# Softmax band selected into 128 columns, parted again on GpSimd behind the transpose, and convolution steps spread over the recurrence

## The reference, cut to what matters

```python
kb, vb = band(k), band(v)                    # block n-1 and block n: 256 keys
s = jnp.einsum('bnqhgd,bnshd->bhgnqs', q, kb) * (B_HEAD_DIM ** -0.5)
dist = q_idx + BLOCK - s_idx                 # 128 x 256
mask = (dist >= 0) & (dist < WINDOW)         # and no key before the first
s = s - slopes * dist
s = jnp.where(mask, s, -jnp.inf)
m = jnp.maximum(jnp.max(s, axis=-1), sink)
p = jnp.exp(s - m)
p = p / (jnp.sum(p, axis=-1) + jnp.exp(sink - m))
o = jnp.einsum('bhgnqs,bnshd->bnqhgd', p, vb)
```

## Time and profile before

| | us |
|---|---|
| median of 3 runs | 1089.53 (1089.48 to 1092.77) |
| the profiled execution, as timed | 1090.27 |
| its span, first to last instruction | 1088.5 |
| TensorE busy | 1064.2 (98%) |
| VectorE busy | 688.7 (63%) |
| ScalarE busy | 532.7 (49%) |
| GpSimd busy | 115.9 (11%) |
| granted TensorE clock | 0.999 |

### The profile page before, as it was taken

The page is one execution under the profiler, slowest core; times in us unless marked ns, Lnnn a source line. Parts: engine busy times, 40 slices in busy tenths (PEclk is TensorE's granted clock), DMA queues, the critical chain, the costliest instruction groups (busy, mean ns, idle before and its releaser), DMA issues.

```text
span 1088.5 us, 19513 instructions
## 1 busy us (share of the span) xinstructions
PE 1064.2 (98%) x7212; PEld 846.5 (78%) x7212; DVE 688.7 (63%) x2081; ACT 532.7 (49%) x1557; POOL 115.9 (11%) x152
## 2 busy tenths in 40 slices
PE   7999999999999999999999999999999999999997
PEld 5877787778778787777887878787787878787885
DVE  5285959584665747576365665757537575758565
ACT  4557675754636454363354535435344555564300
POOL 3413132134100000020000000002000000002210
PEclk9999999999999999999999999999999999999999
DMA  8967475665553626253562551715454343622432
GB/s 282 315 209 262 163 274 195 243 208 183 201 205 109 237 73 235 87 185 98 175 228 93 165 215 46 265 49 185 132 179 157 126 157 128 215 73 63 137 116 77
DMA packets 58430, 183.55 MB, mean 169 GB/s; under 512 B 8480, under 2 KB 21216, under 8 KB 45024
## 3 DMA queue, kind: packets, MB, share of 16 engines
q1 hardware_dynamic: 58192, 182.05, 48.7%
q10 hardware_dynamic: 144, 0.26, 0.1%
HBM read 138.22 MB, written 44.07 MB: 167 GB/s over the span
## 4 chain that ended last, share of the span: by engine, by line
PE 65%; DVE 6%; DMA 2%; issue 1%; ACT 0%; SPq 0%; DVEq 0%
PE bank L849 33%; PE bank L900 10%; PE bank L1137 4%; PE bank L957 2%; PE bank L990 2%; PE bank L972 2%; PE bank L1107 1%; PE bank L1120 1%; PE bank L1117 1%; PE bank L1121 1%; DVE y_cols L1797 1%; DVE y_step L1793 1%; PE bank L1030 1%; PE bank L1045 1%; PE bank L1115 1%
## 5 line engine op out<-in xcount | busy, mean ns | idle before, releaser
L849 PE MATMUL bank<-xr,w 128*128 128x512 f32 x2496 | 653.9, 405 | 7.4 <-DVE xr L1534 7.4
L849 PEld LDWEIGHTS bank<-xr,w 128*128 128x128 f32 x2496 | 449.8, 189 | 101.7 <-issue 9.8
L900 PE MATMUL bank<-wo,y_split 128*128 128x512 f32 x432 | 114.4, 404 | 0.0
L900 PEld LDWEIGHTS bank<-wo,y_split 128*128 128x128 f32 x432 | 77.0, 189 | 14.6 <-issue 0.7
L1582 DVE SCALAR_TENSOR_TENSOR kq<-conv_in,convw_all,kq 128x512 f32<-128x512 f32 x96 | 77.3, 806 | 7.8 <-ACT conv_in L1191 5.8
L1487 ACT ACTIVATE o_scaled<-bank 128x128 f32<-128x128 f32 x64 | 17.7, 277 | 124.5 <-PE bank L1121 124.3
L1353 ACT ACTIVATE score<-score,neg_max 128x256 f32<-128x256 f32 (+1 forms) x128 | 62.7, 493 | 29.0 <-DVE neg_max L1759 29.0
L1919 DVE TENSOR_SCALAR steps<-bank,nb_rk 128x128 f32<-128x128 f32 x64 | 22.3, 348 | 63.9 <-PE bank L1117 63.9
L1922 DVE SCALAR_TENSOR_TENSOR state<-state,cols_all,bank 128x128 f32<-128x128 f32 x64 | 22.2, 347 | 63.2 <-PE bank L1120 63.2
L1793 DVE TENSOR_TENSOR y_step<-blocks,y_cols 128x60 f32<-128x60 f32 (+14 forms) x240 | 50.3, 210 | 12.1 <-DMA blocks<-n_spill 3.3
L783 POOL TENSOR_TENSOR xr<-y_tile,xr 128x256 fp32r<-128x256 f32 x8 | 6.0, 774 | 455.1 <-ACT xr L1172 455.1
(11 more groups left out here) (217 smaller groups left out, 1628.3 us busy)
## 6 DMA issues: line engine op xcount, KB each, us to landing
w<-w_split SPq DMA_DIRECT2D x78, 1024.0 KB, 5.4
w_split<-w SPq DMA_DIRECT2D x26, 1024.0 KB, 5.1
blocks<-n_spill SPq DMA_DIRECT2D x32, 256.0 KB
y_spill<-y_out SPq DMA_DIRECT2D x30, 256.0 KB, 5.8
x_tile<-w_in SPq DMA_DIRECT2D x13, 512.0 KB, 6.1
y_tile<-w_in SPq DMA_DIRECT2D x12, 512.0 KB, 6.4
y_tile<-y_spill SPq DMA_DIRECT2D x12, 512.0 KB, 6.1
x_tile<-x SPq DMA_DIRECT2D x12, 512.0 KB, 3.9
```

Of the source, the lines that this page charges most:

```text
L849: ins = nc.tensor.matmul(bank[JOBS[at].bank][:], w[:, turn % 3, wp, k, :], xr[:, xp, k], start=(step == 0), stop=(step == 3 * KT - 1))
L900: ins = nc.tensor.matmul(bank[JOBS[at].bank][:], y_place(t)[:, yp, k], wo[:, k, wp, half * UNIT:(half + 1) * UNIT], start=(step == 0), sto ...
```

## The change

- `maxima` first copies, in the bank and per head, with a predicate (`recent`, from the distances), those columns of the own block that lie in the window over the past block's columns. 128 columns per row are left, and the bias is 128 wide too, the maximum of both halves of the distances (`dist`); the bias stays 256 wide for slots 0 to 3, because the first block has no past. Maxima, exponentials and divisions work on 128 columns.
- `turns` transposes 128x128 once per cc and hd, all into bank 2; `copy_turned` is one copy of 512 columns per half, into the past half of `score`.
- GpSimd's `part` then makes the two operands for `values`: the turned weights times `tri` into the own half, and times `past` (one less `tri`) in place. Four products of 128x256 per half, one signal per cc. `values` waits for it per cc.
- GpSimd's queue is written out by slot: weight rests in the gaps between parts in the first three slots, those of w_out around the parts of slot 3, x rests before the parts of slots 7 and 11, and the scaled tiles 8 to 10 after the last part.
- `values(n, 1)` moves from before the first chunk to its second third, and `gate_b(n, 1)` behind the first chunk's state.
- `conv` does one step. From slot 3 on there is none before the base inverses and those for k and v of the next slot go one by one into the recurrence: behind `resid` and behind `v_new`, where no job was handled (`conv_gap`), and behind the state. The bias for the next slot (`slopes`) goes behind the third chunk.

```diff
+            def part(n, e):
+                if (n, e) == (0, 0):
+                    pool.wait_ge(part_masks, 1)
+                after(pool, p_copied, n, e + 1)
+                for cc in range(2):
+                    for dst, keep in ((p_own, tri), (p_past, past)):
+                        ins = nc.gpsimd.tensor_tensor(dst[:, cc], p_past[:, cc],
+                                                      keep[:].unsqueeze(1).to_broadcast([P, 2, P]), ALU.mult)
+                    ins.then_inc(p_parted.sem, 1)
...
+            turns = [turn for turn in range(TILES_W) if w_by_pool(turn)]
+            while turns[0] < 9:
+                w_low(turns.pop(0))
+            for n in range(SLOTS):
+                s, i = divmod(n, AH)
+                if n < AH - 1:
+                    w_low(turns.pop(0))
+                    part(n, 0)
+                    w_low(turns.pop(0))
+                    part(n, 1)
+                    for turn in turns[0:2]:
+                        w_low(turns.pop(0))
+                elif n == AH - 1:
+                    for ks in ((0, 1), (2, 3)):
+                        for k in ks:
+                            wo_low(k)
+                        part(n, ks[0] // 2)
+                    for k in range(4, KT - 1):
+                        wo_low(k)
+                else:
+                    if n == AH:
+                        wo_low(KT - 1)
+                    if i == AH - 1 and s < SBS - 1:
+                        x_low(s + 1, 2)
+                        x_low(s + 1, 3)
+                    part(n, 0)
+                    part(n, 1)
+            for t in POOL_TILES:
+                scale_tile(t)
...
             def turns(n, e):
-                s, i = divmod(n, AH)
-                if e == 1 and i == AH - 1 and s < SBS - 1:
-                    after(pe, ba_summed, s + 1, 1)
                 for cc in range(2):
                     after(pe, p_scaled, n, 4 * e + 2 * cc + 2)
-                    if cc == 0:
-                        after(pe, p_scaled, n, 4 * e + 4)
                     for hd in range(2):
-                        for kb in range(1 if (s, e, cc) == (0, 0, 0) else 2):
-                            q = 2 * hd + kb
-                            ins = nc.tensor.transpose(bank[2 + cc][:, q * P:(q + 1) * P],
-                                                      score[:, cc, hd, kb * P:(kb + 1) * P], ident[:])
-                    ins.then_inc(p_turn_done.sem, 1)
+                        q = 2 * cc + hd
+                        ins = nc.tensor.transpose(bank[2][:, q * P:(q + 1) * P], p_own[:, cc, hd], ident[:])
+                ins.then_inc(p_turn_done.sem, 1)
...
                 ins.then_inc(inv_done.sem, 1)
-                values(n, 1)
...
                     fill_to(n, at.chunk(c, 2 / 3))
+                    if c == 0:
+                        values(n, 1)
                     after(pe, v_new_ready, n, c + 1)
...
             def copy_turned(n, e):
-                for cc in range(2):
-                    after(act, p_turn_done, n, 2 * e + cc + 1)
...
+                after(act, p_turn_done, n, e + 1)
+                nc.scalar.activation(p_past, bank[2][:].rearrange("p (c h n) -> p c h n", c=2, h=2), ACT.Copy)\
+                    .then_inc(p_copied.sem, 1)
...
+                lead = (s, e) == (0, 0)
+                for hd in range(2):
+                    both = bank[2 + hd][:].rearrange("p (c k n) -> p c k n", c=2, k=2)[:, int(lead):]
+                    nc.vector.copy_predicated(both[:, :, 0], recent[:].unsqueeze(1).to_broadcast([P, 2 - int(lead), P]),
+                                              both[:, :, 1]).then_inc(packed.sem, 1)
+                after(dve, packed, n, 2 * e + 2)
...
-                convs(n, 0.2)
+                if n < AH - 1:
+                    convs(n, 0.2)
...
-                convs(n, at.p32)
+                convs(n, at.p32, 9 if n < AH - 1 else max(0, 9 * (n + 1) + 3 - conv_place[0]))
                 after_jobs(n, at.step0)
                 for c in range(CH):
                     one = slice(c, c + 1)
-                    if c == 0:
-                        gate_b(n, 1)
                     after(dve, ks_done, n, c + 1)
...
+                    taken = place[0]
                     after_jobs(n, at.chunk(c, 1 / 3))
+                    if place[0] == taken:
+                        conv_gap(n, at.p64 if c == 0 else at.chunk(c - 1))
                     after(dve, tr_done, n, c + 1)
...
+                    taken = place[0]
                     after_jobs(n, at.chunk(c, 2 / 3))
+                    if place[0] == taken:
+                        conv_gap(n, at.p64 if c == 0 else at.chunk(c - 1))
                     after(dve, kv_done, n, c + 1)
...
+                    if c == 0:
+                        gate_b(n, 1)
...
                     after_jobs(n, at.chunk(c, 0.8))
-                    if c < 3:
-                        convs(n, (at.p64, at.chunk(0), 1)[c], 1 if n == AH - 1 and c < 2 else 6)
+                    if n < AH - 1:
+                        if c < 3:
+                            convs(n, (at.p64, at.chunk(0), 1)[c])
+                    elif c < 2:
+                        convs(n, (at.p64, at.chunk(0))[c], 1)
+                    elif c == 2:
+                        convs(n, 1)
+                        if n < SLOTS - 1:
+                            slopes(n + 1)
```

More of the change, by code:

```diff
@@ L940, in scores @@
                 else:
-                    after(pe, p_turned_ready, n, 2)
+                    after(pe, p_copied, n, 1)
                 for cc in range(2):
@@ L1575, in conv @@
                 i = m % AH
-                if half == 0:
+                if step == 0:
                     after(dve, raw_copied, m, c + 1)
                     after(dve, tail_put, m, 1)
-                for step in (0,) if half == 0 else (1, 2):
-                    if step > 0:
-                        after(dve, conv_step, m, 2 * c + step)
-                    ins = nc.vector.scalar_tensor_tensor(acc, conv_in[:, c, step:step + UNIT],
-                                                         convw_all[:, i, c, step:step + 1], acc, ALU.mult, ALU.add)
-                    ins.then_inc(conv_step.sem if step < CONV - 2 else conv_ready.sem, 1)
-                if c == 2 and half == 1:
+                else:
+                    after(dve, conv_step, m, 2 * c + step)
+                ins = nc.vector.scalar_tensor_tensor(acc, conv_in[:, c, step:step + UNIT],
+                                                     convw_all[:, i, c, step:step + 1], acc, ALU.mult, ALU.add)
+                ins.then_inc(conv_step.sem if step < CONV - 2 else conv_ready.sem, 1)
+                if c == 2 and step == CONV - 2:
                     nc.vector.tensor_copy(tails[:, i], conv_in[:, :, UNIT:]).then_inc(tail_saved.sem, 1)
@@ L1698, in _, with convs, conv_gap @@
             conv_place = [0]
-            def convs(n, f, most=6):
-                while conv_place[0] < 6 * SLOTS and most > 0:
-                    m, part = divmod(conv_place[0], 6)
-                    c, half = divmod(part, 2)
+            def convs(n, f, most=9):
+                while conv_place[0] < 9 * SLOTS and most > 0:
+                    m, part = divmod(conv_place[0], 9)
+                    c, step = divmod(part, 3)
                     if JOBS[JOB_AT["qkv"[c], m]].end > n + f + 1e-6:
                         return
-                    conv(m, c, half)
+                    conv(m, c, step)
                     conv_place[0] += 1
                     most -= 1
+            def conv_gap(n, f):
+                if n >= AH - 1:
+                    convs(n, f, 1)
             def split_y(e):
```

72 lines of the change are left out of this document (33 added, 39 removed).

## The result

The changed kernel takes **1112.01 us** (median of 4, 1109.53 to 1113.53) against 1090.94 for the kernel before on the same chip (1089.48 to 1092.77): a ratio of 1.019, 95% interval 1.0162 to 1.0219. Predicted were 1102, 1083 to 1114. The profiled execution took 1111.19 us, its span is 1109.1 against 1088.5: 20.6 us more.

What follows compares the result with a forecast made beforehand. TensorE, busy 98% of the span, was taken as the bound. Waits of 15.5 + 6.0 - 0.4 + 4.4 = 25.5 us against 13.1 saved gave +12.4, 1102.7 on the profiled execution, so 1102 us; range 1083 to 1114.

Steps and rivals of the forecast that it cites:

- The forecast case: Whole kernel: new TensorE waits exceed the transposes saved, point 1102 us, own range 1095 to 1110; chance 0.60.
- Heavier: Rival: each GpSimd product holds VectorE for its whole length, or gap convolution steps delay `v_new` and state; 1112 to 1118, chance 0.10.
- Waits of line 1067: First half, TensorE waiting for VectorE's transposed base inverses: GpSimd's products make these later, 15.5 us more over the slots.
- The price of a product: VectorE's base inverses: each GpSimd product beside them costs 0.44 us, 1.8 us for four.
- The rival with half the price: Base steps lose only 0.22 us per GpSimd product; waits +15 against 13.1 saved, 1091.5 us; chance 0.14.
- First chunks: Slots 0 to 2, line 1117: TensorE waits for a later `resid`, 2.0 us three times, 6.0 us.
- Slot 15: GpSimd's queue delays tile 8 and so tile 10's load: 5.2 us more, less 0.8 us at second transposes, 4.4.
- Saved: TensorE: 120 fewer transposes of the weights at 0.109 us each, 13.1 us less.
- I cost them at nothing: Convolution steps moved behind the inverses' reads and into the recurrence cost nothing; without cover, up to 0.77 us a step.
- the saving stands: Rival: products fall where VectorE waits or base inverses start earlier; 1081 us with tile 10 late, 1077 without; chance 0.16.

## Why the prediction was right, and where it was off

The forecast case came true, slower by more waits than the transposes are worth, and 1112.0 lies inside the range. Its point was 10 us too low, and the sum's own range ended at 1110. "Heavier" had named 1112 to 1118, so the measured number is met there too, but for another reason: its mechanism is excluded below. On the profiled executions it said +12.4 and 20.6 came: the waits came out 1.4 smaller than their sum of 25.5, and what was missing is the clock (6.8), a smaller saving (1.2) and the last store (1.2).

- *Waits of line 1067 (+15.5).* Measured 20.3 - 3.8 = 16.5. Slots 0 to 2 waited 2.79, 2.68 and 2.65 (forecast 2.5), 7 and 11 2.44 and 2.48 (2.8), 12 and 15 1.71 and 1.36 (1.4 each), and 4, 5, 6, 8, 9, 10, 13, 14 nothing. The error was slot 3, 4.2 for 2.0; that the sum is only 1.0 off is in part luck, since the 1.3 forecast for slots 4, 13 and 14 did not come. The step had the four products "follow the second group of wo", 12 inside; in the written order the third group follows directly behind them and falls inside too: 16.
- *The price of a product (0.44).* 0.47 in slot 3, 0.48 in slot 5. The rival with half the price is out, and so is "heavier": with 0.74 us lost for each, slot 5's inverses would take 10.5, not 9.4, and the convolution steps in the gaps don't show at TensorE: it waits 0.5 us in all for the state (0.4 before) and not for `v_new`. The Trainium skill, "SBUF — State Buffer", section "SBUF: two separate sides", has the loser blocked for the other's whole instruction; the trace differs in what that costs, since the two engines alternate and VectorE's own step is part of each turn (0.20 alone, 0.67 beside a product).
- *First chunks (+6.0).* Measured 4.3. Without the second half's products 0.7 of each 1.4 us stays, so GpSimd is half of the cause; the rest was not taken apart.
- *Slot 15 (+4.4).* 5.41 instead of 0.28, less the 0.8: 4.3. Store 2.62 and load 3.63 us as worked out. Moving tile 8 removed it.
- *Saved (-13.1).* 15.0 in the transposes themselves, 3.1 given back at line 1149: 11.9. The step took them from a chain and did not ask what stands behind the moved values.
- *"I cost them at nothing"* (convolution steps in the gaps): right for their cost; what they save in front of the base inverses is worth up to 9.4 us here, the clock included.
- *The failed step is one that isn't there.* The prediction priced a wait as its length. In the kernel before no wait after the start is over 1.0 us and the clock does not fall before the last matmuls; in the changed one there are waits of 2.4 to 5.4, and behind four of them PE works at 1.2 GHz: 6.8 us. The Trainium skill's page "TensorE: Matmul & The Clock Gate", section "What's actually happening", says that activity releases a throttle that idling brings back; the runs here agree, and filling the waits is what shows it.
- A wait of 1.5 us for a weight load in slot 14 was not foreseen, nor the later landing of the last store; neither was taken apart, and two small waits of before that went (lines 957 and 972 at the start of slot 4, 0.8 and 1.0) make up for the first.

The rival "the saving stands" fell twice: products cost what slot 3 had shown, and even with all of them gone the saving isn't there, used up by slot 3's w_out products, slot 15 and the clock. Why the clock falls behind one wait and not behind its like stays open.

## What to carry to other kernels

Price work given to an idle GpSimd by what VectorE does at that moment: small two-input steps beside it lost 0.47 us per product of 0.7 us, and the products cost more than the TensorE time they freed. Where TensorE is busy 98%, a new wait of some two microseconds or more (1.8 was the shortest here) can have two prices, its length and up to half of the several microseconds behind it at 1.2 GHz, of which a later wait may give a part back; look at the granted clock behind each wait before trusting a sum, and when a wait can't be removed, a filler of useless matmuls is worth trying (7.3 us here). Moving the waiting place later in the plan hands the wait on to whatever the plan had behind it.

## What the runs showed of the hardware that I had not expected

- The stretches at 1.2 GHz were 3.41, 6.83 or 10.24 us long, and did not stand behind each equal wait: in the profiled execution of the changed kernel the waits of 2.7 us in slots 0 to 2 had none, in the run with tile 8 first the same waits had all three, and waits of 2.4 us in slots 7 and 11 had one each.
- The same kernel's times go with its clock: with later places one execution took 1105.19 us at a mean of 0.994, three 1113 to 1115 at 0.980 to 0.983. Not all scatter is this: 23 executions of the kernel before lie between 1089.35 and 1097.24 us, all at 0.996 or more.
- A slower TensorE hides waits: in the run with tile 8 first, behind stretches at 1.2 GHz, the residual waits of slots 0 to 2 were 0.4 to 0.7 us instead of 1.4, so a trace with more low clock can show fewer waits.
